# Expert rows gathered to every second and every eighth partition, and turned with a matrix that picks them

## What is computed

```
def expert_choice_ffn(x, p):
    B, L, D = x.shape
    cap = CAPACITY_FACTOR * L // N_EXPERTS          # 64 latent rows, 16 context rows
    aff = jax.nn.softmax((x @ p['w_router']).astype(jnp.float32), axis=-1)
    g, idx = lax.top_k(jnp.swapaxes(aff, 1, 2), cap)
    xs = x[bidx, idx]
    h = (jax.nn.silu(jnp.einsum('becd,edf->becf', xs, p['w_gate']))
         * jnp.einsum('becd,edf->becf', xs, p['w_up']))
    y = jnp.einsum('becf,efd->becd', h, p['w_down']) * g[..., None].astype(x.dtype)
    return jnp.zeros_like(x).at[bidx, idx].add(y)
```

## Time and profile before

| | us |
| --- | --- |
| median of 3 runs | 2505.74 |
| lowest and highest | 2502.99, 2505.90 |
| the profiled execution's own time | 2506.81 |
| its span, first to last instruction | 2504.6 |
| PE busy in the span | 2336.8 |

### The profile page before, as it was taken

One profiled execution on the slowest core, in us unless ns is written; L12 is line 12 of the kernel. 1 busy time (PEld: TensorE's weight loads), 2 busy tenths in 40 slices (PEclk: granted clock), 3 DMA queues, 4 the chain that ended last, 5 costly groups with the idle time before them and its releaser, 6 DMA issues.

```text
span 2504.6 us, 56885 instructions
## 1 busy us (share of the span) xinstructions
PE 2336.8 (93%) x26284; PEld 1518.9 (61%) x26284; DVE 593.5 (24%) x906; ACT 333.1 (13%) x707; POOL 268.5 (11%) x370
## 2 busy tenths in 40 slices
PE   5999999999999999999999489999999999998997
PEld 3468887555555565554445376666666666666663
DVE  4124341344444434321125400000000000000001
ACT  3011111122322323210012100000000000000000
POOL 0156760100000000000110000000000000000000
PEclk9999999999999999999998599999999999999999
DMA  9913114865556311242422889999999999999995
GB/s 370 351 65 91 55 47 89 277 218 201 180 198 212 123 38 54 79 165 80 162 101 106 276 344 374 402 398 398 400 402 402 397 398 397 395 397 389 408 400 202
DMA packets 181495, 628.75 MB, mean 251 GB/s; under 512 B 12522, under 2 KB 89028, under 8 KB 150852
## 3 DMA queue, kind: packets, MB, share of 16 engines
q1 hardware_dynamic: 163008, 585.04, 61.1%
q0 software_dynamic: 3072, 20.97, 3.6%
q10 hardware_dynamic: 15188, 19.19, 2.3%
HBM read 600.72 MB, written 24.44 MB: 250 GB/s over the span
## 4 chain that ended last, share of the span: by engine, by line
PE 74%; DMA 16%; DVE 4%; issue 2%; ACT 2%; SPq 1%; ACTq 1%; POOL 0%; DVEq 0%; POOLq 0%
PE PS L1493 17%; PE PS L1312 14%; PE PS L1403 11%; DMA work<-in_w_gate 9%; PE PS L1507 9%; PE PS L1128 7%; DMA hT_<-in_w_gate 3%; PE PS L1070 3%; PE PS L1005 3%; DVE work L1802 2%; PE PS L1340 2%; DMA work<-in_w_up 1%; DMA work<-in_w_ada 1%; PE PS L1300 1%; PE PS L1032 1%
## 5 line engine op out<-in xcount | busy, mean ns | idle before, releaser
L1493 PE MATMUL PS<-hT_,work 128*64 128x80 f32 x14336 | 539.6, 237 | 57.0 <-issue 25.7
L1493 PEld LDWEIGHTS PS<-hT_,work 128*64 128x64 f32 x14336 | 520.0, 141 | 112.5 <-issue 68.9
L1312 PE MATMUL PS<-hT_,work 128*128 128x512 f32 (+1 forms) x1536 | 441.5, 437 | 0.0
L1312 PEld LDWEIGHTS PS<-hT_,work 128*128 128x128 f32 x1536 | 224.7, 192 | 158.1 <-issue 158.1
L1507 PE MATMUL PS<-work,hT_ 128*32 128x512 f32 (+1 forms) x2544 | 301.4, 596 | 4.5 <-issue 3.9
L1403 PE MATMUL PS<-work,mixT_ 128*128 128x512 f32 x640 | 283.4, 604 | 0.0
L1918 DVE TENSOR_TENSOR hT_<-PS,hT_ 128x480 f32<-128x480 f32 x16 | 10.5, 658 | 953.4 <-ACT hT_ L988 953.4
L1403 PEld LDWEIGHTS PS<-work,mixT_ 128*128 128x128 f32 x640 | 123.3, 194 | 151.3 <-issue 151.3
L1128 PE MATMUL PS<-work,hT_ 128*128 128x256 f32 x960 | 212.7, 380 | 0.8 <-DMA work<-in_w_in 0.8
L1128 PEld LDWEIGHTS PS<-work,hT_ 128*128 128x128 f32 x960 | 180.4, 190 | 26.4 <-DMA work<-in_w_in 1.2
L1507 PEld LDWEIGHTS PS<-work,hT_ 128*32 128x32 f32 (+1 forms) x2544 | 71.9, 105 | 146.9 <-issue 134.4
(11 more groups left out here) (251 smaller groups left out, 1731.4 us busy)
## 6 DMA issues: line engine op xcount, KB each, us to landing
work<-in_w_up SPq DMA_DIRECT2D x57, 2048.0 KB, 29.8
work<-in_w_down SPq DMA_DIRECT2D x56, 2048.0 KB, 35.8
work<-in_w_gate SPq DMA_DIRECT2D x55, 2048.0 KB, 32.9
work<-in_w_ada SPq DMA_DIRECT2D x48, 2048.0 KB, 13.0
work<-in_w_in SPq DMA_DIRECT2D x80, 512.0 KB, 4.7
hT_<-in_w_gate SPq DMA_DIRECT2D x9, 2048.0 KB, 35.0
work<-in_w_out SPq DMA_DIRECT2D x4, 4096.0 KB, 13.2
hT_<-in_w_down SPq DMA_DIRECT2D x8, 2048.0 KB, 30.3
```

The costliest lines, as they stand in the source:

```text
L1312: last = pe.matmul(bank(2 * which, n, col), w_chunk[chunk % NW][:, HD * (k % 8):HD * (k % 8) + HD], hT[:, k, col:col + n], start=(k == 0), ...
L1493: last = pe.matmul(hidden_at(u, f)[64 * h:64 * h + 64, :], w[:, k % 4, f // 2, f % 2, 64 * h:64 * h + 64], xsT[s][:, k, :], start=opens, s ...
```

## The change

Four things change.

- The buffer `xs` now spans all 128 partitions. A gather is two indirect DMAs. The first takes the 64 latent rows to the partitions 0, 2, 4 to 126, the second the 16 context rows to 1, 9, 17 to 121. Each has its own column of row numbers (`row_from`, `ctx_from`). The context's numbers are first copied by DVE from partitions 64 to 79 to partitions 0 to 15 (`ctx_row`). `s_gath` now counts 32 for an expert, and `s_row` counts 2.
- A turn is no longer a transpose of 80 partitions but an fp32 matmul. Its stationary operand is the full 128x128 piece of `xs`, and its moving operand is `slot_of`, 128x80, whose column `i` holds a one in the partition of slot `i`.
- POOL builds `slot_of` from the identity matrix (two copies) and clears both `xs` buffers (two memsets of 128x2048), since the partitions that no row fills are read too. It does so after it has seen the router's last matmul (`s_logit`) and before it waits for the row numbers (`s_slot`).
- PE waits once for `slot_of` (`s_slot_of`).

```
-        row_from = [take(1, SLOTS).bitcast(U32) for _ in range(2)]
+        row_from = [take(1, CAP_L).bitcast(U32) for _ in range(2)]
+        ctx_row = take(16, CAP_C).bitcast(U32)
+        ctx_from = [take(1, CAP_C).bitcast(U32) for _ in range(2)]
...
-        xs = [mixT_[0:SLOTS, D * (1 + i):D * (2 + i)] for i in range(2)]
+        xs = [mixT_[:, D * (1 + i):D * (2 + i)] for i in range(2)]
+        slot_of = diag[:, 0:SLOTS]
...
-                    last = turn(bank(7, SLOTS, (k - 4 * b) * SLOTS), xs[s][:, k * P:(k + 1) * P], SLOTS)
+                    last = pe.matmul(bank(7, SLOTS, (k - 4 * b) * SLOTS), xs[s][:, k * P:(k + 1) * P], slot_of, start=True, stop=True)
...
-            pe.wait_ge(s_gath[0], 16)
+            pe.wait_ge(s_slot_of, 1)
+            pe.wait_ge(s_gath[0], 32)
...
+            ch.link(dve.tensor_copy(ctx_row, bank(2, 16, 16)[CAP_L:SLOTS, :]))
             dve.tensor_copy(slot_row, bank(2, 16, 16)[0:SLOTS, :]).then_inc(s_slot, 1)
...
-                pool.tensor_copy(row_from[s], rows_of(e)).then_inc(s_row, 1)
-                pool.wait_ge(s_row, e + 1)
+                pool.tensor_copy(row_from[s], rows_of(e)[0:CAP_L]).then_inc(s_row, 1)
+                pool.tensor_copy(ctx_from[s], rows_of(e, ctx_row)).then_inc(s_row, 1)
+                pool.wait_ge(s_row, 2 * e + 2)
                 apart(pool)
-                pool.indirect_dma_start(xs[s], None, h2_d, bass.IndirectOffsetOnAxis(ap=row_from[s], axis=0))\
-                    .then_inc(s_gath[s], 16)
+                for at_, rows in ((row_from[s], slice(0, P, 2)), (ctx_from[s], slice(1, P, 8))):
+                    pool.indirect_dma_start(xs[s][rows], None, h2_d,
+                                            bass.IndirectOffsetOnAxis(ap=at_, axis=0)).then_inc(s_gath[s], 16)
...
+            pool.wait_ge(s_logit, TT)
+            for s in range(2):
+                ch.link(pool.memset(xs[s], 0.0))
+            ch.link(pool.tensor_copy(slot_of[:, 0:CAP_L], ident[:, 0:P:2]))
+            pool.tensor_copy(slot_of[:, CAP_L:SLOTS], ident[:, 1:P:8]).then_inc(s_slot_of, 1)
+            pool.wait_ge(s_slot_of, 1)
             pool.wait_ge(s_slot, 1)
```

10 lines of the change are left out of this document (5 added, 5 removed).

## The result

The changed kernel takes 2,491.7 us (median of 7 runs), the kernel before beside it 2,505.9 us. The ratio is 0.9934, with a 95% interval of 0.9921 to 0.9947: 14 us faster, where 2 us were forecast. The profiled execution took 2,492.9 us with a span of 2,491.1.

The account below looks back on a forecast made before the run. The prediction took DMA to bound the 13 experts after the first four, with PE binding after the change. Its terms, -9.0 + 3.4 + 3.7 + 0 = -1.9 us, gave 2,503.8 us beside 2,505.7; range 2,490 to 2,513 and a us or two.

Parts of the forecast that it names:

- I take 1.7: Expert stage: spreading a gather's rows saves the DMA engines 1.7 of 2.3 us an expert, leaving 65.2.
- half of the ways into SBUF: First two gathers: 217 GB/s, half the weights' rate, looks like half the SBUF paths, not a cost per row.
- the context's 16 may not: Second transfer: the 64 latent rows gain, the context's 16 may not, as only transfers spanning all partitions reach all ports.
- PE needs 63.8 + 1.7 = 65.5 us an expert: Expert stage: PE's measured 63.8 us plus 1.7 for longer turns makes 65.5, against 65.2 for the DMA engines.
- term 1: The 13 experts' stretch: from 860.5 to 851.5 us, PE binding; -9.0 us.
- term 2: Start of the stage: eight blocks of turns, of experts 1 and 2, cost 0.43 us more each; +3.4 us.
- Term 3: Expert 0's four blocks of turns at 1.2 GHz cost 0.92 us more each, all on the path; +3.7 us.
- Term 4: First gather: extra copies and a later issue balance faster flow; 0 us, between -1.5 and +1.5.
- first rival: Expert stage: PE's unnamed stalls go with the slow gathers, 1 us an expert; given as 2,493 us, chance 22%.
- The second: Gathers: the indirect form is what is slow, so spreading saves under 0.7 us; 2,512.8 us, chance 15%.
- the fourth: Turns: matmuls do not overlap their weight loads, PE needs 69.2 us an expert; about 2,557 us, chance 6%.
- The third: Gathers: the fullest engine's share counts, six rows for eight saving 0.6 us an expert; 2,505.7 us, chance 12%.

Follow-up runs that it names:

- e1_turn128: The changed kernel with turns made 128x128 transposes, whose columns ACT picks in two copies; 2,484.2 us.
- e9_low64: The changed kernel with 128x128 transposes, latents in partitions 0 to 63, and no context transfer in 14 experts; 2,502.8 us.
- e10_mid64: The changed kernel with 128x128 transposes, latents in partitions 32 to 95, and no context transfer in 14 experts; 2,468.6 us.
- e5_nogather: The kernel before without the gathers of experts 2 to 15; 2,452.3 us.
- e14_nogather_mm: The changed kernel, matmul turns kept, without the gathers of experts 2 to 15; 2,479.0 us.
- e2_packed: The changed kernel with rows packed in partitions 0 to 63 and 64 to 79, still two transfers and matmul turns; 2,522.3 us.
- e4_matmul: The kernel before with only the turns changed, to fp32 matmuls; 2,507.8 us.
- e16: The changed kernel with the context's rows in partitions 33, 37 to 93 and the picking matrix to match; 2,483.9 us.
- e11_all128: The changed kernel with 128x128 transposes and one gather of 128 rows, 48 of them unread copies of row 0; 2,485.3 us.
- e6_shift24: The kernel before with its one transfer of 80 rows sent to partitions 24 to 103, turned by 128x128 transposes; 2,501.4 us.
- e7: The kernel before with gathered rows in partitions 24 to 103, 128x128 transposes, and the scatter's results in 32 to 111; 2,503.5 us.
- e15_scsplit: The changed kernel with 128x128 transposes, context rows at 33, 37 to 93, and the scatter in two transfers; 2,477.9 us.

## Why the prediction was wrong where it was

**What bounds the kernel.** Right. DMA set the pace from the fifth expert on, and in the changed kernel PE does.

**The gather's saving.** The step "I take 1.7" holds: 1.6 us by the slices, and with PE out of the way (e1_turn128) the DMA engines' need is 65.2 us an expert, as the prediction had it. Its reason, "half of the ways into SBUF", is confirmed in kind by e9_low64 and e10_mid64. Its size isn't: 64 rows at 0 to 63 cost 29.7 / 12 = 2.5 us more than at 32 to 95. Four more rows on the fullest port of the Trainium skill's map at 423 / 16 = 26.4 GB/s would be 32 KB, 1.2 us. The uneven load costs twice that, and why isn't settled. That "the context's 16 may not" gain was right in its result, 0.7 us still lost a gather, but the cause is their place, not the second transfer.

**PE's need: the step that failed.** It reads "PE needs 63.8 + 1.7 = 65.5 us an expert", and it is 64.67. What was wrong above all is the 63.8. "In the first four PE waits 8.9 us in all, and no DMA is among the releasers" was true, and the conclusion "So PE alone needs 63.8 us an expert" was not. e5_nogather takes 61.9 us in the same four experts. The packed gathers' price for PE, 1.9 us an expert, was already in the figure to which I added the turns, though no wait named them. The spread gathers cost PE 64.6 - 64.35 = 0.25 us an expert there (the changed kernel less e14_nogather_mm).

The turns' 1.7 us were too small, too: 2.45 by the first four experts and 2.5 by the blocks, for a block displaces 1.05 us and not 0.85. So the sum was 61.9 + 1.9 + 1.7 where the runs have 61.9 + 0.25 + 2.45 = 64.6. The two errors had opposite signs, and that the miss is only 0.9 us an expert is luck.

Over the 13 experts PE's account is, in us:

| | before | after |
| --- | --- | --- |
| gate and up matmuls | 500.5 | 487.3 |
| down matmuls | 296.0 | 295.7 |
| turns | 25.8 | 58.2 |
| waits for DMA | 34.6 | 2.4 |
| unnamed waits | 19.4 | 14.4 |
| less what overlaps | -15.8 | -17.3 |
| stretch | 860.5 | 840.7 |

The first row is from these groups, of the kernel before and of the changed one:

```profile
L1493 PE MATMUL PS<-hT_,work 128*64 128x80 f32 x11648 | 438.1, 237 | 46.2 <-DMA work<-in_w_up 16.1 <-issue 15.6 <-DMA work<-in_w_gate 14.2
...
L1493 PE MATMUL PS<-hT_ 128*64 128x80 f32 x1664 | 62.4, 237 | 4.0 <-DMA hT_<-in_w_gate 3.8 <-issue 0.3
```

```profile
L1497 PE MATMUL PS<-hT_,work 128*64 128x80 f32 x11648 | 426.8, 234 | 13.4 <-issue 11.4 <-DMA work<-in_w_gate 1.7
...
L1497 PE MATMUL PS<-hT_ 128*64 128x80 f32 x1664 | 60.5, 233 | 0.7 <-DMA hT_<-in_w_gate 0.7
```

The same 13,312 records are busy 13 us less. This is no need of PE's that went away: 12.2 of the 13.2 us lie behind the fourth expert, where the clock differs. The kernel before in the two parts of the stretch (us, busy time and count of PE, PEld, DVE, ACT, POOL, clock, DMA share, GB/s), and one piece of it behind a wait:

```profile
1542.60:1797.70 255.10, 246.13 (x4932) 171.69 (x4928) 21.56 (x32) 9.64 (x25) 11.08 (x16) 1.00 1.01 398
1797.70:2403.20 605.50, 559.94 (x11096) 397.42 (x11092) 48.50 (x72) 21.71 (x56) 23.71 (x34) 0.98 1.00 398
```

```profile
2161.32 6.29 PE L1493 MATMUL PS<-hT_,work 128*64 128x80 f32 x128 [3.42 <-DMA work<-in_w_up]
```

The granted clock is 0.98 behind the fourth expert and 1.00 in the changed kernel. After a wait of 3.42 us for weights the same 128 records take 6.29 us, which take 4.65 at full clock. PE lost that time while the DMA engines set the pace. In the first four experts, at a clock of 1.00 in both, the gate and up matmuls are busy 151.2 and 150.2 us, and what fell are the unnamed waits, by 5.4 us or 1.35 an expert.

The stretch fell by 19.9 us where term 1 said 9.0, and that difference is nearly all of the miss.

**Terms 2 and 3.** From expert 0's first piece to the stretch's start it is 112.9 us for 110.9, 2.0 us more, for term 2's 3.4. Neither figure can be told from scatter: the same part takes 109.6 to 111.7 us in the four other kernels with matmul turns (e2, e4, e14, e16) and 110.6 in e5_nogather with the turns of before. So no run shows the price of these eight blocks. Term 3 was 3.7 and measured 4.8, and 10.1 us from first turn to first piece is what all kernels with matmul turns take. A block is busy 1.97 us at a granted clock of 0.50, not 1.72. The rows that I took as bounds did not bound: 0.81 us for eight records with 16 columns and 0.94 with 128, where a block with 80 displaces 1.05. Both came from a row of alike records, and a block stands alone between other matmuls. That would explain it; no run shows it. The denser turns did not visibly bring the clock up earlier: the first two pieces take 11.55 us, for 10.94, and 10.39 to 11.51 in the other four kernels with matmul turns.

**Term 4.** It was 0, between -1.5 and +1.5. From issue to first turn the changed kernel takes 6.0 us for 9.1. But e4_matmul and e5_nogather, whose first gather is that of the kernel before, take 7.05 and 6.7 us, and e14_nogather_mm, whose first gather is that of the changed kernel, takes 6.45. So between 0.2 and 3 us are gained, against at most 0.4 of POOL's and DVE's new copies, and nothing finer can be said than that term 4 was not far off.

**The rivals.** The first comes nearest: "PE's stalls go too", 2,493 us, and 838.5 us for the stretch at its full amount. Its mechanism, that PE's stalls go with the slow gathers, is what the first four experts show: 1.35 us an expert less of unnamed waits, for its 1. Its gain from the clock at the start is not to be seen, and its 838.5 us are near the 840.7 because its errors cancel as well: 1 us of stalls where 1.9 - 0.25 = 1.65 went, and 1.7 us for the turns where they cost 2.45. The second falls (e9_low64 against e10_mid64). So does the fourth: a block displaces 1.05 us, under its 1.2. The third's idea, the fullest share, orders most of these kernels rightly, but its price of 0.6 us for two rows was too small by more than half, and the fullest port is not all that counts: e11_all128 puts eight rows on every port and costs (839.1 - 809.8) / 12 = 2.4 us a gather over e5_nogather, which its 1.05 MB take at full rate, and e9_low64, with eight rows on eight ports and none on the others, costs 3.7.

**Chances and range.** The forecast's own range, 2,500 to 2,509, missed the time, and the whole range, from 2,490, held it near its edge, by the first rival and by the two errors that partly cancel. Only 35% were given to a time that is clearly faster, and 43% to no change that can be told. The 22% for the first rival were too few: of its reasons against, neither "the scatter stays" nor "the full amount needs everything at once" spoke against the part that counts here. A base time measured with the disturbance running was the forecast's weakest number, and the forecast's own range had nothing for it.

## What to carry over

When an edit takes a transfer's cost away, don't take an engine's own pace from a stretch in which that transfer still runs, even if no wait names it; leave the transfer out once and look. Lay rows so that every port of the Trainium skill's map gets as many as the others (32 to 95 or every second partition for 64 rows, every fourth from 33 for 16); half of them on each side of partition 64 is not enough by itself (e6_shift24). Do so before paying for a scheme that needs another operation to undo it: here 128x128 transposes with ACT picking the columns undo it for less than fp32 matmuls do. Here short blocks of a new form between other matmuls cost more than long rows of the nearest forms said. And when a group's records grow shorter, look at the granted clock before calling it a gain of the engine.

## What the runs showed of the hardware

- One gather of 64 rows of 8 KB beside a stream of weights costs 2.5 us more at partitions 0 to 63 than at 32 to 95, and 16 rows cost 1.2 us at every eighth partition and 0.5 at 33, 37 to 93. By the Trainium skill's map and an estimate of 423 / 16 = 26.4 GB/s for a port, the fullest port's bytes explain 1.2 of the first 2.5 us and 0.3 of the second 0.7.
- Splitting one gather into 64 and 16 packed rows costs 10 us over 12 gathers (e2_packed against e4_matmul). Splitting a scatter leaves the stretch as it was, 829.0 us for 830.5 (e15_scsplit); the 6 us between the medians are unexplained.
- PE's unnamed waits follow how the gathers are laid, with no wait for a transfer in sight. In the first four experts they are 7.6 to 9.7 us in the six kernels that by the Trainium skill's map put eight rows on some ports and at most four on the others (before, e2, e4, e6, e7, e9), and 2.7 to 4.9 in the eleven with evener gathers or none. That instructions are fetched through the same DMA engines (the queue q8 above) would fit; no run shows it.
- PE's granted clock fell, to 0.50 from 1,892 to 1,896 us for one, behind waits for weights in the kernel before (0.98 on the mean from 1,797.7 to 2,403.2 us), and records were longer by it: 6.29 us for 4.65.
- An fp32 matmul turn of 128 partitions to 80 columns displaces 0.26 us at full clock, a transpose of 80 partitions 0.10. A block of four 128x128 transposes displaces 0.59 us:

```profile
1588.78 0.66 PE L1010 MATMUL PS<-consts,mixT_ 128*128 128x128 f32 x4
1589.37 0.85 PE L1498 MATMUL PS<-hT_,work 128*64 128x80 f32 x18
```
